# The z columns of a hybrid trunk's input projection, computed once for all heads by Strassen ahead of the heads

## The chip, the core and the metric

The kernel runs on one core of one Trainium2 chip. The metric is the time of one execution on the device in microseconds (us), the median of repeated runs. A NeuronCore has five engines with one instruction queue each: PE (TensorE, the matmuls), DVE (VectorE), ACT (ScalarE), POOL (GpSimd) and SP (SyncE, which only issues DMA transfers here). They meet only at semaphores.

## The reference, cut to what matters

One decoder layer over 1040 tokens (16 meta tokens and 1024 others) of width 1024. RMSNorm gives u; one projection gives everything the three branches read; z is 1024 columns of it and only gates the SSM branch.

```python
u = rmsnorm(h, norm_w[layer])
proj = jnp.einsum('bld,de->ble', u, w_in[layer])
(q, k, v, g_attn, c_b, c_c, c_h, g_conv, z, xbc, dt) = jnp.split(proj, IN_SPLIT_POINTS, axis=-1)
...
y_ssm = ssd_branch(z, xbc, dt, ...)      # ends in gated_group_rmsnorm(y, z, w): y * silu(z), then RMSNorm by group
...
h = h + jnp.einsum('ble,ed->bld', y, w_out[layer])
return rmsnorm(h, final_norm_w)[:, N_META:]
```

## The kernel before, in words

All data are float32. A product is made of three matmuls of rounded halves, high times high, high times low and low times high: ACT writes the high half (a cast to float32r), DVE or POOL the low half (source minus high). u is kept in SBUF for the whole kernel as `u_hi` and `u_lo`, 8 tiles of 128 columns of the model by 1040 tokens.

The program has three parts. Every engine walks the same written list of steps (`AHEAD`, then `BODY` for three heads, then `LAST`) and does those that are its own, in that order; nothing is reordered at run time, and semaphores alone hold an engine back.

1. The token stage (`ahead()`): for each of 9 token tiles `x_square` (ACT), `x_mean` (DVE), `x_power` (POOL), `x_scale` (DVE), `x_turn` (PE, eight transposes into PSUM), `x_high` (ACT) and `x_low` (DVE). Two tiles have PSUM room of their own (`u_ps`). Between the turns of the last tiles PE projects the first head's K and Q; `BEHIND` holds the other pieces of Q, K, V and the small dt products.
2. Four heads. In each, attention, and then a scan over 9 chunks (steps `chunk`, `decay`, `scan`, `carry`, `norm`, `ssm_out`). Between their steps `filler` deals out half pieces of projection (`project`: 12 matmuls of 342 to 512 columns), so that PE has work while the others answer. The head's 256 z columns are 8 steps `z` on PE, one for each 128 tokens, 24 matmuls of 256 columns each: three between the last attention steps, one ahead of `chunk` 0, and four as filler of the first chunks. ACT takes the tanh of each, DVE gates it into `z_n`. `PAUSE` puts empty units behind them.
3. The output projection, 2048 by 1024, by Strassen's method in seven products (`M_11` ... `M_22`, 8 slots each; `multiply` makes 3 matmuls of 512 columns for each of 4 token tiles).

DMA transfers are issued by SP in the order of the list: `load` for the weights of a projected tile (512 KB), `decay_load` for the scan, `x_load` and so on.

## Time and profile before

| | |
|---|---|
| time, median of 3 runs | 1036.84 us (1036.62 to 1036.87) |
| span of the profiled execution | 1035.9 us |
| PE busy | 1010.1 us (98%) |
| DVE, ACT, POOL busy | 622.6, 443.3, 253.3 us |
| matmuls | 6177 |

The span runs from the first to the last instruction of one profiled execution; the page gives no other time of that execution, and the median of the runs without a profile is 0.9 us longer. A busy share says how full an engine is, not who is waited for; for that there are the waits and the chain that ended last, a walk back from the last instruction to whatever released each step.

### The profile page before, as it was taken

What the parts mean: (1) busy time and instruction counts of PE and PEld (TensorE: products, weight loads), DVE (VectorE), ACT (ScalarE), POOL (GpSimd) and SP (SyncE); (2) the same over time, 40 slices, a digit from 0 to 9 for tenths busy, and PEclk for the clock granted to TensorE, in tenths of its full rate; (3) what the DMA queues carried; (4) which work ended last, traced back from release to release, by engine and by line L of the source; (5) the groups of instructions that cost most, each with busy time, mean ns of one, the idle gap of its engine ahead of it and who ended that gap; (6) DMA issues with size and microseconds to landing.
All of it is one profiled execution on the core that took longest, in us unless ns stands there. A gap on an engine that the chain in (4) does not pass through costs nothing.

```text
span 1035.9 us, 16326 instructions
## 1 busy us (share of the span) xinstructions
PE 1010.1 (98%) x6177; PEld 923.2 (89%) x6177; DVE 622.6 (60%) x1199; ACT 443.3 (43%) x1020; POOL 253.3 (24%) x222
## 2 busy tenths in 40 slices
PE   3999999999999999999999999999999999999997
PEld 3889989998999999989999999899999898888885
DVE  7555766446257664462576644625766536798866
ACT  6333444343434343434343344343433544543555
POOL 3012331233223412332224133322241330000002
PEclk8999999999999999999999999999999999999999
DMA  8012322221143232211422322114223203994313
GB/s 271 1 45 82 102 80 78 69 62 52 45 129 102 66 88 72 62 43 40 144 91 69 92 76 62 42 41 143 74 75 98 77 24 106 364 385 143 101 52 163
DMA packets 105945, 101.22 MB, mean 98 GB/s; under 512 B 6022, under 2 KB 79852, under 8 KB 105868
## 3 DMA queue, kind: packets, MB, share of 16 engines
q1 hardware_dynamic: 105868, 100.18, 30.2%
q8 instruction: 50, 0.82, 0.3%
q14 instruction: 27, 0.22, 0.1%
HBM read 79.11 MB, written 21.05 MB: 97 GB/s over the span
## 4 chain that ended last, share of the span: by engine, by line
PE 95%; DVE 2%; ACT 1%; issue 1%; DMA 1%; POOL 0%; DVEq 0%; SPq 0%; ACTq 0%
PE ps L1614 51%; PE ps L1623 15%; PE ps L1815 9%; PE ps L1599 5%; PE ps L1780 3%; PE ps L1829 2%; PE ps L1758 2%; PE ps L1759 2%; PE ps L1831 1%; PE ps L1835 1%; PE ps L1706 1%; PE ps L1781 1%; PE ps L1800 1%; DMA conv_u<-in_norm_w 1%; PE ps L1762 0%
## 5 line engine op out<-in xcount | busy, mean ns | idle before, releaser
L1614 PE MATMUL ps<-u_hi,w_hi 128*128 128x348 f32 (+3 forms) x1024 | 364.3, 356 | 1.8 <-POOL w_lo L908 1.8
L1614 PE MATMUL ps<-u_lo,w_hi 128*128 128x348 f32 (+3 forms) x1024 | 348.1, 340 | 0.0
L1614 PE MATMUL ps<-u_hi,w_lo 128*128 128x348 f32 (+3 forms) x1024 | 347.4, 339 | 0.0
L908 POOL TENSOR_TENSOR w_lo<-w_raw,w_hi 128x1024 fp32r<-128x1024 f32 (+1 forms) x56 | 122.8, 2193 | 343.7 <-ACT w_hi L998 271.7
L1614 PEld LDWEIGHTS ps<-u_hi,w_hi 128*128 128x128 f32 x1024 | 193.9, 189 | 13.5 <-POOL w_lo L908 2.1
L1614 PEld LDWEIGHTS ps<-u_hi,w_lo 128*128 128x128 f32 x1024 | 193.2, 189 | 11.0
L1614 PEld LDWEIGHTS ps<-u_lo,w_hi 128*128 128x128 f32 x1024 | 193.6, 189 | 10.3
L899 POOL TENSOR_TENSOR small<-small,m_half 128x1 f32<-128x1 f32 (+2 forms) x57 | 41.3, 727 | 332.0 <-DVE small L1553 143.0
L1388 DVE TENSOR_REDUCE small<-ps 128x1 f32<-128x144 f32 (+7 forms) x64 | 49.6, 774 | 90.4 <-PE ps L1762 89.9
L1815 PE MATMUL ps<-w_hi,u_hi 128*128 128x256 f32 x256 | 73.1, 286 | 0.0
L1815 PE MATMUL ps<-w_lo,u_hi 128*128 128x256 f32 x256 | 72.0, 281 | 0.0
L1815 PE MATMUL ps<-w_hi,u_lo 128*128 128x256 f32 x256 | 71.9, 281 | 0.0
L1090 ACT ACTIVATE work<-ps,small 128x144 f32<-128x144 f32 (+7 forms) x64 | 48.1, 751 | 53.8 <-DVE small L1388 53.8
L1122 ACT ACTIVATE y_n<-y_n,small 128x256 f32<-128x256 f32 x32 | 16.3, 509 | 116.5 <-POOL small L899 116.5
L1599 PE MATMUL ps<-ident,work 128*128 128x128 f32 (+2 forms) x369 | 55.7, 285 | 7.0 <-DVE work L1224 7.0
L1623 PE MATMUL ps<-q_hl 128*128 128x512 f32 x264 | 62.1, 389 | 0.0
L1623 PEld LDWEIGHTS ps<-q_hl 128*128 128x128 f32 x264 | 49.6, 188 | 10.3
L1599 PEld LDWEIGHTS ps<-ident,work 128*128 128x128 f32 (+2 forms) x369 | 43.7, 141 | 10.6 <-DVE work L1224 8.5
L1464 DVE TENSOR_TENSOR lm_buf<-lm_buf,cbm 128x512 f32<-128x512 f32 x32 | 22.1, 691 | 50.4 <-PE ps L1835 40.4
L998 ACT CAST w_hi<-w_raw 128x1024 fp32r<-128x1024 f32 x48 | 50.0, 1041 | 0.0
L1815 PEld LDWEIGHTS ps<-w_hi,u_hi 128*128 128x128 f32 x256 | 48.1, 188 | 1.3 <-issue 1.3
L1108 ACT ACTIVATE lm_buf<-acum_b,sg 128x128 f32<-128x128 f32 x128 | 40.8, 390 | 18.2 <-DMA acum_b<-acum_scratch 14.4
(302 smaller groups left out, 1741.1 us busy)
## 6 DMA issues: line engine op xcount, KB each, us to landing
w_raw<-in_w_in SPq DMA_DIRECT2D x56, 512.0 KB, 4.1
...
```

What stands on the lines that cost most here:

```text
L899: return eng.tensor_tensor(to[0:rows_, n:n + w], of[0:rows_, n:n + w], m_half[0:rows_, 0:w], ALU.pow)
L908: eng.tensor_tensor(w_lo[:, a % 2, ks, :], w_raw[:, a % 2, ks, :], w_hi[:, a % 2, ks, :].bitcast(F32), ALU.subtract).then_inc(w_lo_ok, 1)
L998: eng.copy(w_hi[:, b, :, :], w_raw[:, b, :, :]).then_inc(w_hi_ok, 1)
L1090: eng.activation(prob[m][:, 0:nk], s_ps[:, 0:nk], ACT.Exp, bias=mx[:, m:m + 1], accum_out=psum_e[:, s % 2, m:m + 1]).then_inc(exp_ok, 1)
L1108: ins = eng.activation(lmat[:, a % 2, r, :], acum_b[:, a % 2, r, :], ACT.Relu, bias=sg[:, 1, a, r:r + 1], scale=-1.0)
L1388: eng.tensor_reduce(mx[:, m:m + 1], s_ps[:, 0:nk], AX.X, ALU.max, negate=True).then_inc(max_ok, 1)
L1464: eng.tensor_tensor(lmat[:, b, :, :], lmat[:, b, :, :], cbm[:, b, :].unsqueeze(1).to_broadcast([P, R, P]), ALU.mult).then_inc(g_ok, 1)
L1599: return eng.transpose(dst, src, ident[0:n, 0:n])
L1614: ins = eng.matmul(dst, w[:, k, 0:m], u[:, k, cols], start=(k == 0 and n == 0), stop=(k == KD - 1 and n == 2))
L1623: ins = eng.matmul(ps[:, BANKS[n // KS][t], :], y[:, at], w, start=(begins and m == 0), stop=(ends and m == 2), skip_group_check=True)
L1780: eng.matmul(o_ps[:, P:2 * P], a_t[:, n, :], v_blk[:, n, :], start=(n == 0), stop=False)
L1815: ins = eng.matmul(pb[p % 2][:, 0:GW], u[:, k, ca:cb], w[:, :, k, :], start=(k == 0 and n == 0), stop=(k == KD - 1 and n == 2))
```

## The change

z no longer belongs to the heads. Between the token stage and the first head the whole of z, 1024 tokens by 1024 columns over a depth of 1024, is computed in Strassen's seven products of 512 by 512 by 512: `M_11`, `M_12`, `M_S2`, `M_S1`, `M_S3`, `M_S4`, `M_22`, each of 4 slots (a slot is one 128 deep step for 4 token tiles: 12 matmuls of 512 columns, `z_multiply`). The first two, 8 slots, are the steps `z_early` and need only u; the other five, slots 8 to 27, are in `z_run` and need sums of quarters of u (`s1`, `s2`, `s3`, each split into high and low) and of quarters of the weights (`z_sum`). Results are gated (`z_tanh`, `z_gate`) and stored to DRAM (`z_store`); each head reads its 1 MB back by one `z_load`. The heads' `z` steps are gone, the pieces of `TCB` stand in their places around the end of attention, and `PAUSE` is 1. In the token stage each tile now goes in two halves through one PSUM bank each, no projection stands between the turns, the splitting of z's weights stands among its steps, and Q, K, V of the first head come behind z (`PRE`). The lists `Z_ACT` and `Z_DVE`, not shown, write out the order of ACT and DVE in `z_run`.

```diff
+ZK = KD // 2
+Z_SLOTS = 7 * ZK
+ZX_BANKS, ZY_BANKS = (0, 1, 4, 7), (5, 6, 2, 3)
+Z_BANKS = (ZX_BANKS, ZY_BANKS, ZX_BANKS, ZX_BANKS, ZY_BANKS, ZX_BANKS, ZY_BANKS)
+Z_BLOCKS = {"T3": (0, 0), "T4": (1, 0), "T1": (0, 1), "T2": (1, 1)}
+Z_OF = ("T3", "T4", "T2", "T1", "T3", "T2", "T4")
+Z_TURNED = 8
+Z_OUT = ((0, 0), (1, 1), (0, 1), (1, 0))
+Z_READ = (M_12, M_S2, M_S3, M_S4, M_22)
+Z_EARLY = [(p, t, j) for p in (M_11, M_12) for t in range(4) for j in range(ZK)]
+Z_PER_TURN = 1
...
+def ahead():
...
+    early = list(Z_EARLY)
+    for r in range(-3, CH):
+        if 0 <= r:
+            out += [("x_high", (r, 0)), ("x_high", (r, 1))]
+        if r + 1 in range(CH):
+            out.append(("x_scale", r + 1))
+        if r + 2 in range(CH):
+            out += [("x_mean", r + 2), ("x_power", r + 2)]
+        out += [(name, arg) for name, arg, at in BETWEEN if at == r]
+        if r + 3 in range(CH):
+            out.append(("x_square", r + 3))
+        if 0 <= r:
+            out += [("x_low", (r, 0)), ("x_low", (r, 1))]
+        if r >= 5:
+            out.append(("s1", r - 5))
+        if r + 1 in range(CH):
+            out.append(("x_turn", (r + 1, 0)))
+            out += [("z_early", early.pop(0)) for _ in range(0)]
+            out.append(("x_turn", (r + 1, 1)))
+            out += [("z_early", early.pop(0)) for _ in range(Z_PER_TURN - 1 if r > 0 else 0)]
+    out += [("z_early", e) for e in early]
+    return [(name, arg, 1) for name, arg in out]
+
+
+BETWEEN = [("z_high", 0, 0), ("z_high", 1, 0), ("z_low", 0, 0), ("z_low", 1, 0), ("z_high", 2, 1), ("z_high", 3, 1), ("z_low", 2, 1), ("z_low", 3, 1),
+           ("z_high", 4, 2), ("z_low", 4, 2), ("z_high", 5, 3), ("z_low", 5, 3), ("z_high", 6, 4), ("z_low", 6, 4), ("z_high", 7, 5), ("z_low", 7, 5),
...
         if s == QB:
-            add("split", TZ1)
-            add("load", TCB)
-            add("load", TCC)
+            add("z_load")
...
-    add("z", 1)
...
-    units = [[("z", a, 0)] for a in range(5, QB + 1)]
-    units[-1].append(("split", TCB, 0))
-    units += [[]] * PAUSE
...
+    add("o_mean", 1)
+    emit(conv[0])
+    spare(1)
+    add("o_scale", 1)
+    emit(conv[1])
+    spare(2)
+    emit(conv[2])
+    add("attn_out", 1)
+    add("store_attn")
+    spare(9)
+    add("decay_load", 1)
+    add("decay_load", 2)
+    emit(conv[3])
+    add("chunk", 0)
+    add("decay", 1)
+    units = [[]] * PAUSE + conv[4:]
+    jobs = [(n + PAUSE - 4, job) for n, job in jobs]
+    if not last:
+        units += half_pieces([TQ, TK, TV], 1)[0]
...
-PAUSE = 4
+PAUSE = 1
...
+            def z_run():
+                iteration(-1, [("s2", 0, 1), ("s2", 1, 1), ("z_sum", ("T2", 1), 1), ("z_sum", ("T3", 0), 1), ("z_sum", ("T3", 1), 1),
+                               *[("s3", (M_S3, k), 1) for k in range(ZK)], ("z_sum", ("T4", 0), 1), ("z_sum", ("T4", 1), 1),
+                               *[("s3", (M_S4, k), 1) for k in range(ZK)]])
...
+                    elif step == "z_low":
+                        high, low = z_ring(a)
+                        eng.wait_ge(z_hi_ok, a + 1)
+                        eng.tensor_tensor(low, z_src(a), high.bitcast(F32), ALU.subtract).then_inc(z_lo1_ok, 1)
+                    elif step == "z_sum":
+                        name, half = a
+                        x, y, done = {"T1": ("T1", "T3", 0), "T2": ("T2", "T1", 1 + half), "T3": ("T2", "T3", 3 + half), "T4": ("T4", "T2", 3 + half)}[name]
+                        if name in ("T1", "T2"):
+                            eng.wait_ge(z_in[name], 32)
+                        if done:
+                            eng.wait_ge(z_sum_ok, done)
+                    elif step == "s3":
+
+                        p, k = a
+                        cols = slice(META + HALF, L) if p == M_S3 else slice(META, META + HALF)
+                        q = (M_S3, M_S4).index(p) * ZK + k
+                        if q == 0:
+                            eng.wait_ge(z_out_ok, 4)
+                            eng.wait_ge(s2d_ok, 2)
+                        if q >= 2:
+                            eng.wait_ge(s_lo_ok[M_S3 if q - 2 < ZK else M_S4], (q - 2) % ZK + 1)
+                        own(eng, eng.tensor_tensor(s_f[q % 2], u_hi[:, ZK + k, cols].bitcast(F32), s2_f[:, k, :], ALU.subtract))
+                        eng.tensor_tensor(s_f[q % 2], s_f[q % 2], u_lo[:, ZK + k, cols].bitcast(F32), ALU.add).then_inc(s3_ok, 1)
...
+                    elif step == "z_acc":
+
+                        o, t = a
...
+                        eng.copy(z_tmp[o][t], ps[:, ZX_BANKS[t], :]).then_inc(z_acc_ok, 1)
...
-                        eng.wait_ge(x_tr, a + 1)
-                        eng.copy(u_hi[:, :, ca:cb], u_ps[a % 2].rearrange("p (k n) -> p k n", k=KD)[:, :, 0:cb - ca]).then_inc(u_hi_ok, 1)
+                        eng.wait_ge(x_tr, 2 * a + h + 1)
+                        if a >= 5 and h == 0:
+                            eng.copy(s1_f[a - 5], u_ps[0])
+                        eng.copy(u_hi[:, ZK * h:ZK * (h + 1), ca:cb], u_ps[h].rearrange("p (k n) -> p k n", k=ZK)[:, :, 0:cb - ca]).then_inc(u_hi_ok, 1)
...
+                    elif step == "s1":
+
+                        eng.wait_ge(u_hi_ok, 2 * (a + 5) + 2)
+                        eng.tensor_tensor(s1_f[a], u_ps[1], s1_f[a], ALU.add).then_inc(s1_ok, 1)
...
-                            eng.wait_ge(bank_free[p % 2], it * (PPI // 2) + p // 2 + 2)
+                            eng.wait_ge(z_n_in, 16 * (it + 2))
...
+            def z_multiply(n, t):
+                p, j = divmod(n, ZK)
+                hi_u, lo_u = z_u(p, j, t)
+                hi_w, lo_w = z_ring(n)
+                terms = [(hi_u, hi_w), (hi_u, lo_w), (lo_u, hi_w)]
+                for m, (u, w) in enumerate(terms):
+                    ins = eng.matmul(ps[:, Z_BANKS[p][t], :], u, w, start=(p in BEGINS and j == 0 and m == 0),
+                                     stop=(j == ZK - 1 and m == 2), skip_group_check=True)
+                return ins
+            def z_run():
+                for n in range(Z_TURNED, Z_SLOTS):
+                    p, j = divmod(n, ZK)
+                    eng.wait_ge(z_lo_ok, n - Z_TURNED + 1)
+                    if p in (M_S3, M_S4):
+                        eng.wait_ge(s_lo_ok[p], j + 1)
+                    if p == M_S1 and j == 0:
+                        eng.wait_ge(s_lo_ok[p], 4)
...
+                        ins = z_multiply(n, t)
+                        if j == ZK - 1 and p in Z_READ:
+                            ins.then_inc(z_bank, 1)
+                    if not (j == ZK - 1 and p in Z_READ):
+                        ins.then_inc(z_k, 1)
...
-                        if a >= 2:
-                            eng.wait_ge(u_lo_ok, a - 1)
-                        for k in range(KD):
-                            ins = turn(u_ps[a % 2][:, k * P:k * P + n], x_buf[a][0:n, k * P:(k + 1) * P], n)
+                        if a >= 1:
+                            eng.wait_ge(u_lo_ok, 2 * a + h - 1)
+                        if a >= 6:
+                            eng.wait_ge(s1_ok, a - 5)
+                        for k in range(ZK):
+                            ins = turn(u_ps[h][:, k * P:k * P + n], x_buf[a][0:n, (ZK * h + k) * P:(ZK * h + k + 1) * P], n)
...
```

Three places of the order that the rows are read at. PE in the token stage, before; `work` and `lm_buf` hold the token tiles, x8 is eight transposes in a row:

```order
L1614 MATMUL ps<-u_hi,w_hi 128x348
L1614 MATMUL ps<-u_lo,w_hi 128x348
L1614 MATMUL ps<-u_hi,w_lo 128x348
L1599 MATMUL ps<-ident,lm_buf 128x128 x8
L1614 MATMUL ps<-u_hi,w_hi 128x348
L1614 MATMUL ps<-u_lo,w_hi 128x348
```

and after, from the program's start:

```order
L1870 MATMUL ps<-ident,ys 128x16 x8
L1870 MATMUL ps<-ident,work 128x128 x64
L1904 MATMUL ps<-w_hi,u_hi 128x512
L1904 MATMUL ps<-w_lo,u_hi 128x512
L1904 MATMUL ps<-w_hi,u_lo 128x512
L1904 MATMUL ps<-w_hi,u_hi 128x512
```

Before, 36 matmuls of the first head's K and Q stand between the turns of the last tiles; after, all 72 turns stand together and the first matmul of z comes behind the last of them.

POOL from the token stage's end to the first head, before (row L915 is part of the token stage):

```order
L915 TENSOR_TENSOR wd<-conv_g,wd 128x8x16
L899 TENSOR_TENSOR small<-small,m_half 128x1 x3
L908 TENSOR_TENSOR w_lo<-w_raw,w_hi 128x1024 x4
L944 TENSOR_TENSOR work<-work,acum_b 128x512
L908 TENSOR_TENSOR w_lo<-w_raw,w_hi 128x1024
```

and after, from the fifth sum of weights on; `lot` holds two sums of u at a time and `w_raw` the sum S2; a row of 1024 elements is half of a weight quarter:

```order
L1072 TENSOR_TENSOR th_tile<-th_tile,conv_b_s 128x1024
L1072 TENSOR_TENSOR conv_u<-conv_y,conv_u 128x1024
L1072 TENSOR_TENSOR acum_b<-th_tile,acum_b 128x1024
L1089 TENSOR_TENSOR lot<-u_hi,w_raw 128x512
L1090 TENSOR_TENSOR lot<-lot,u_lo 128x512
L1089 TENSOR_TENSOR lot<-u_hi,w_raw 128x512
L1090 TENSOR_TENSOR lot<-lot,u_lo 128x512
L1089 TENSOR_TENSOR lot<-u_hi,w_raw 128x512
```

In this stretch DVE has, after:

```order
L1487 TENSOR_TENSOR s_ys<-xdt,s_work 128x4x128
L1487 TENSOR_TENSOR s_ys<-xdd,s_work 128x4x128
L1487 TENSOR_TENSOR s_ys<-xd,s_work 128x4x128
L1487 TENSOR_TENSOR s_ys<-y_n,s_work 128x4x128
L1497 TENSOR_TENSOR w_lo<-conv_g,w_hi 128x512
L1493 TENSOR_TENSOR s_work<-lot,s_work 128x512
L1497 TENSOR_TENSOR w_lo<-conv_g,w_hi 128x512
L1493 TENSOR_TENSOR s_work<-lot,s_work 128x512
L1497 TENSOR_TENSOR w_lo<-conv_b_s,w_hi 128x512 x2
L1493 TENSOR_TENSOR s_work<-lot,s_work 128x512
L1497 TENSOR_TENSOR w_lo<-conv_u,w_hi 128x512
```

Every row here and in POOL's list reads two operands, both in SBUF. Before, POOL had nothing between the token stage and the weights of V; after, it has sixteen 512-element rows (`s3`) and two of 1024 (`T4`) that stand behind DVE's gate of the first result.

PE at the start of the last head's scan, before; `xdd` is what POOL makes of chunk 0:

```order
L1815 MATMUL ps<-w_hi,u_lo 128x256
L1599 MATMUL ps<-ident,work 16x128 x3
L1599 MATMUL ps<-ident,work 128x128 x3
L1800 MATMUL ps<-work 128x128
L1815 MATMUL ps<-w_hi,u_hi 128x256
L1815 MATMUL ps<-w_lo,u_hi 128x256
...
L1815 MATMUL ps<-w_hi,u_lo 128x256
L1835 MATMUL ps<-xdd,b_n 128x256
L1815 MATMUL ps<-w_hi,u_hi 128x256
```

and after:

```order
L1885 MATMUL ps<-u_hi,w_lo 128x512
L1870 MATMUL ps<-ident,work 16x128 x3
L1870 MATMUL ps<-ident,work 128x128 x3
L2116 MATMUL ps<-work 128x128
L2136 MATMUL ps<-xdd,lot 128x256
L1885 MATMUL ps<-u_hi,w_hi 128x342
L1885 MATMUL ps<-u_lo,w_hi 128x342
```

Before, a z step of 24 matmuls stood between the transposes of chunk 1 and the first product of the scan; after, nothing does. It is so in all four heads.

## Rows read from the trace of the kernel before

**Rows 1.** The page, its head and the line of busy times.
```profile
span 1035.9 us, 16326 instructions
...
PE 1010.1 (98%) x6177; PEld 923.2 (89%) x6177; DVE 622.6 (60%) x1199; ACT 443.3 (43%) x1020; POOL 253.3 (24%) x222
```

**Rows 2.** The waits of PE, whole execution.
```profile
PE ps L1599 <- DVE work L1224: 7.0, 4, 2.6
PE ps L1614 <- POOL w_lo L908: 1.8, 1, 1.8
```

**Rows 3.** The chain that ended last, in order of time: start, length, what.
```profile
25.64 3.29 PE ps L1614 x12
29.80 1.91 PE ps L1614 x12
...
36.23 2.79 PE ps L1614 x12
...
170.23 2.84 PE ps L1815 x24
```

**Rows 4.** The same chain, asked for from 885 us on.
```profile
884.96 143.99 PE ps L1623 x635
```

**Rows 5.** Timeline of PE, token stage: start, length, what.
```profile
23.67 1.97 PE L1599 MATMUL ps<-ident,work 128*128 128x128 f32 x8 [1.91 <-DVE work L1224]
...
35.20 1.04 PE L1599 MATMUL ps<-ident,ys 128*128 128x128 f32 x8
```

**Rows 6.** Timeline of ACT, token stage.
```profile
15.49 1.01 ACT L1011 CAST u_hi<-ps 128x1024 fp32r<-128x1024 f32 x1
16.39 1.06 ACT L1004 ACTIVATE conv_y<-work 128x1024 f32<-128x1024 f32 x1
...
17.45 1.03 ACT L998 CAST w_hi<-w_raw 128x1024 fp32r<-128x1024 f32 x1
```

**Rows 7.** Stretches: busy time by engine, clock, DMA share, GB/s.
```profile
0.00:12.00 12.00, 2.42 (x15) 2.34 (x16) 5.94 (x13) 6.08 (x10) 3.95 (x19) 1.00 0.82 273
12.00:18.00 6.00, 3.62 (x19) 2.59 (x17) 4.56 (x7) 5.41 (x8) 2.34 (x3) 1.00 1.08 348
```

**Rows 8.** Groups by shape: count, busy us, mean ns of one.
```profile
L1201 DVE TENSOR_TENSOR q_hl<-ys,q_hl 128x512 fp32r<-128x512 f32 x10 | 6.9, 694 | 1.7 <-ACT q_hl L976 1.7
```

**Rows 9.** Timeline of POOL, attention of the first head.
```profile
127.30 2.38 POOL L908 TENSOR_TENSOR w_lo<-w_raw,w_hi 128x1024 fp32r<-128x1024 f32 x1 [1.53 <-ACT w_hi L998]
129.65 2.31 POOL L944 TENSOR_TENSOR work<-work,acum_b 128x512 f32<-128x512 f32 x1
132.03 2.29 POOL L944 TENSOR_TENSOR work<-work 128x512 f32<-128x512 f32 x1
...
148.76 1.28 POOL L944 TENSOR_TENSOR acum_b<-acum_b,work 128x512 f32<-128x512 f32 x1
```

**Rows 10.** Timeline of DVE, same stretch.
```profile
125.99 1.30 DVE L1367 SCALAR_TENSOR_TENSOR work<-lm_buf,par_cw,work 128x1040 f32<-128x1040 f32 x1
...
128.34 2.44 DVE L1367 SCALAR_TENSOR_TENSOR work<-lm_buf,par_cw,work 128x1040 f32<-128x1040 f32 x1
...
131.94 1.24 DVE L1376 SCALAR_TENSOR_TENSOR work<-th_tile,work 128x1040 f32<-128x1040 f32 x1 [0.56 <-ACT th_tile L1076]
```

**Rows 11.** Timeline of DVE, token stage.
```profile
20.85 1.37 DVE L1298 TENSOR_TENSOR w_lo<-w_raw,w_hi 128x512 fp32r<-128x512 f32 x1
```

**Rows 12.** Timeline of PE, start of the first head's scan.
```profile
173.56 0.39 PE L1800 MATMUL ps<-work 128*128 128x128 f32 x2
...
176.72 0.69 PE L1835 MATMUL ps<-xdd,b_n 16*128 16x256 f32 x2
```

**Rows 13.** Timeline of DVE, same stretch.
```profile
173.52 0.42 DVE L1473 SCALAR_TENSOR_TENSOR work<-th_piece,ps 128x256 f32<-128x256 f32 x1 [0.77 <-ACT th_piece L1115]
173.86 0.41 DVE L1453 TENSOR_TENSOR xdt<-ps,sg 16x256 f32<-16x256 f32 x1
```

**Rows 14.** Timeline of POOL, same stretch.
```profile
174.34 1.18 POOL L923 TENSOR_TENSOR xdd<-xdt,sg 16x256 f32<-16x256 f32 x2 [10.07 <-DVE xdt L1453]
```

More of the change, by code:

```diff
@@ L155, with z_done, z_kept @@
 assert len(FIRST) == first_piece(TXS0)
-def ahead():
-    out = [("x_load", 0, 1), ("x_load", 1, 1), ("norm_load", 0, 1), ("x_load", 2, 1), ("x_load", 3, 1), ("load", 0, 1),
-           ("x_load", 4, 1), ("load", 1, 1), ("w_dt_load", 0, 1)]
-    out += [("x_load", a, 1) for a in range(5, CH)] + [("params_load", 0, 1)]
-    for r in range(-3, CH):
-        for name, lead in PIPE:
-            if 0 <= r + lead < CH:
-                out.append((name, r + lead, 1))
-        out += [(name, arg, 1) for name, arg, at in BETWEEN if at == r]
-    return out + [(name, arg, 1) for name, arg in BEHIND]
+ZK = KD // 2
[9 more added lines that the diff above has]
+Z_PER_TURN = 1
+def z_done(n):
+    p, j = divmod(n, ZK)
+    if p == M_11:
+        return "z_k", 1
+    if p in Z_READ and (j == ZK - 1 or p == M_12):
+        return "z_bank", 4 * (Z_READ.index(p) + 1)
+    return "z_k", 1 + sum(1 for m in range(2 * ZK, n + 1) if not (m % ZK == ZK - 1 and m // ZK in Z_READ))
+def z_kept(o, t):
+    return 4 * (0, 3, 1).index(o) + t + 1
 def piece(t, tc):
@@ L172, in piece @@
     return [("project", (p, 0)), ("project", (p, 1)), ("piece", p)]
-PIPE = (("x_high", 0), ("x_square", 3), ("x_scale", 1), ("x_mean", 2), ("x_low", 0), ("x_power", 2), ("x_turn", 1))
-BETWEEN = [("split", 0, 1), ("split_low", 0, 2), ("split", 1, 2), ("split_low", 1, 3), ("load", 2, 3), ("w_dt", 0, 3),
-           ("project", (first_piece(TK), 0), 4), ("project", (first_piece(TK), 1), 5),
-           ("project", (first_piece(TQ), 0), 6), ("project", (first_piece(TQ), 1), 7), ("dt_piece", 0, 7)]
@@ L411, in build @@
         k_hl = sb("k_hl", [P, 2, LP], F32R)
+        with nc.sbuf_tensor("s_work", [P, 4, 4 * HALF], F32R) as s_work:
+            pass
         work = sb("work", [P, 8324])
@@ L480, in build @@
         v_meta = sb("v_meta", [P, P])
+        with nc.sbuf_tensor("s_ys", [P, 4 * HALF], F32R) as s_ys:
+            pass
         ys = sb("ys", [P, 2, T])
```

397 lines of the change are left out of this document (279 added, 118 removed).

## The prediction

> **What bounds the kernel now.** I read the page first: PE is busy for 98% of the span and the others for 60% at most [rows 1], so matmul time counts unless a wait takes its place. PE's waits say where it is not full: it waits 7.0 us for the scaled token tiles and once 1.8 us for the low weights of V [rows 2]; the heads hold next to none. So two things decide: how much PE work goes, and whether PE can be kept as full in a stage that did not exist.
>
> The chain that ended last gives PE's pace, which durations do not, since matmuls overlap. A z step of 24 matmuls takes 2.84 us, 0.1185 us for 256 columns. A half piece of 12 takes 1.91 us at about 348 columns and 2.79 at 512 [rows 3]. In the output projection, which has the shape that z gets, 635 matmuls take 143.99 us, 0.2268 each [rows 4].
>
> **PE's work.** Removed: 32 z steps, 32 x 2.84 = 90.9 us. Added: 7 products x 4 slots x 12 = 336 matmuls of 512 columns, at the output projection's pace 76.2 us; at the half pieces' pace (2.79 / 12) it would be 78.1. I take the first, since the loop is the same. By the Trainium skill ("TensorE: Matmul & The Clock Gate", section "Wait — 56ns, not 53.3ns?") a warm matmul of 512 columns comes every 215.7 ns, which would make 72.5 us; no row here shows that pace. Strassen and wider matmuls thus save 14.7 us.
>
> **What the token stage hid.** Before, PE did 36 matmuls of K and Q between the last turns. The last turn starts at 35.20 [rows 5] and hands over 0.8 later, at 36.0; from there to the end are 999.9 us. After, the same 36 matmuls stand behind z and cost 1.91 + 1.91 + 2.79 = 6.6 us, which nothing hides. Before, the first 12 of them took 3.29 us instead of 1.91 [rows 3], as PE came out of the sparse stage at half its clock (1.2 GHz); z's first matmuls meet the same, and since this is now behind the 36.0 mark it costs a further 1.6.
>
> **When the turns end after.** A walk in order of each list. ACT casts a 1024-element tile in 0.90, and squares one in 1.06, start to start [rows 6]; two halves cost about 1.05, one 512-element cast 0.5. DVE's operations on 512 elements take 0.69, 0.6 start to start [rows 8]. ACT's first `z_high` needs block T3, the seventh transfer, 3.2 MB in; 273 GB/s over 12 us moved 3.3 MB [rows 7], so it starts at 12.3, and `x_square` 3 and tile 1's casts stand behind it: two `z_high` and the square end at 14.4. Tile 1 (casts, two `z_high`, square) takes 3.1, to 17.5. Tile 2 waits for T4, the twelfth transfer, 5.8 MB, at 19.3 by the 348 GB/s of the next stretch [rows 7], and ends at 20.9. Tiles 3 and 4 take 2.7 each: 26.3. From tile 5 on another loop is longer, because PSUM has one bank for each half and `s1` reads it too. Tile 5's copy, casts, `x_low` and `s1` end at 29.4. For tiles 6 and 7 the loop is four turns at their slow pace 1.0 (half of the 1.97 in [rows 5]), copy and cast 1.05, second cast 0.55, `x_low` 0.65, `s1` 0.65, signals 0.15: 4.05 each, 37.5. Eight turns of tile 8 end at 39.4.
>
> To that comes what POOL does to DVE. Both were asked for operations with two SBUF operands at once in [rows 9] and [rows 10]: DVE's tap, 1.30 when alone, takes 2.44 and ends 1.1 after POOL's 2.38; POOL's sum, 1.28 when alone, then takes 2.31 and ends 1.2 after DVE's; the next again waits for DVE's 1.24. They take turns. In the token stage too DVE's 0.69 became 1.37 beside POOL [rows 11]. The Trainium skill ("SBUF — State Buffer", section "🔬 SBUF: two separate sides") has such a rule: the port pair that the two share is locked for a whole instruction and the other blocks. By that rule, the trace agrees. Here `z_sum` of T1's second half (2.4 us) and `x_scale` 8 become ready together behind `x_power` 8. If DVE loses, the turns of tile 8 end at 41.6. I take 40.6, the middle, since no row says who wins such a start.
>
> **Inside z's seven products.** From E, the end of the turns: the slow start 1.6, then `M_11` and `M_12` of 48 x 0.2268 = 10.9 each; slots 8 to 11 (2.72 each) end at E + 34.3, slot 20 is due 8 x 2.72 later, at E + 56.1. `M_12`'s first tile is done at E + 15.2; behind it DVE has 20 operations until `z_gate` (0, 3), 12.6 us, E + 27.8. Only then may POOL begin `s3`, since the sums share `lot` with the tanh. Up to `z_low` 20, which slot 20 needs, POOL has 20 units of 512 elements and DVE 20 low halves, all with two SBUF operands, each side often needing the other's last. Taking turns, a pair costs 1.28 + 0.69 less the 0.16 by which two turns overlapped (131.96 to 134.32 is 2.36, against 1.28 + 1.24) = 1.81; 20 x 1.81 = 36.2, so `z_low` 20 ends at E + 64.0 and PE has waited 8 us by then. Were there no turns to take, POOL's 20 x 1.28 + 0.6 would end at E + 54.0, in time: zero. I take 7, as DVE is not always there to take its turn. Behind slot 20 all is done early. ACT has 60 operations of about 0.5 in the stage, which it hides; the DMA stores, the second read of T2 (issued about E + 45) and the heads' `z_load` (1 MB, some 20 us ahead of its use) hide too; the first head's weights are split during `M_22`, 11 us of PE work against 7.
>
> **In the heads.** `scan` 0 now follows the turns of chunk 1 at once. It needs `xdd`, made by POOL from DVE's `xdt`. Before, the PE went on to a z step after the turns at about 173.7 and the scan began at 176.72 [rows 12]. DVE's `xdt` stood behind a z gate and began at 173.86 [rows 13]; POOL's first `xdd` began at 174.34 and lasted half of 1.18 [rows 14]. Without the gate it ends at 174.5: PE waits 0.8 us, in four heads 3.2. If it does not wait in this way, zero; if the loss of cover costs the whole chain anew, 1.5 each. The last head's filler falls from 28 units to 16 over nine chunks; scan c - 1, the masked product, mean, power and scaling take about 2.2 us ahead of `ssm_out`, against one half piece of 1.9 between. Some 0.3 in six chunks, less 1.1 us that PE was idle there before: 0.7.
>
> **Sum.** 40.6 + 999.9 - 90.9 + 6.6 + 1.6 + 76.2 + 7.0 + 3.2 + 0.7 = 1044.9 us of span, against 1035.9 before; with the 0.9 by which the median stands above the span, 1045.8.
>
> **Rivals.** A change under 0.2% (2.1 us) cannot be told from none here.
> *The two engines do not collide in z.* For it: [rows 9] has DVE work with larger operations, and a DVE idle at the right time costs nothing. Against it: both lists are full there. Turns end at 39.4 and z waits 0.2: 1037.7, at the edge of no change.
> *The token stage is shorter.* My 39.4 is a sum of loops that I lengthened step by step; should ACT not wait for T3 and T4 and tiles 5 to 7 go at ACT's 2.7, the turns end at 33.5, and with no collision the time is 1031.8: faster. It decides from turns that end by 36.5 without collision, and by 29 with it, which I think impossible.
> *The filler is missed.* Each of the 32 chunk steps loses 0.25 us with fewer units between: 8 us more, 1053.8. Against it: before, chunks with empty units went by with hardly a wait.
> *No Strassen gain:* if wide matmuls with a changing stationary came at the half pieces' pace and each token tile's change of bank cost 0.08 (112 times 0.08 = 9 us), the time would be near 1056; [rows 4] has such changes and speaks against it.
>
> **How the numbers follow.** Forecast (collision, 1041 to 1050): 0.52. No collision: 0.16. Short token stage: 0.17. Filler missed or dear matmuls: 0.15. Range 1036.5 to 1053: it leaves out most of the faster case and half of the slowest. Faster takes the short token stage and a hundredth of the others, 0.18; same takes most of the second case, 0.12; slower 0.70.
>
> **What would show it.** Right: no matmul between the turns, the last turn ending near 40; slots 16 to 20 waiting for DVE's low halves, DVE's 0.69 and POOL's 1.28 stretched to about twice; four waits of 0.8 at the scan's first product; z's 336 matmuls near 76 us. Wrong: a token stage that ends by 36, or POOL and DVE at their lone durations in z.

## The result, and the profile of the changed kernel

The changed kernel takes 1056.14 us (median of 4 runs, 1055.10 to 1057.76) against 1036.86 for the kernel before (1036.62 to 1037.24): a ratio of 1.0186 (in brackets, here and below, the 95% interval: [1.0171, 1.0200]). It is slower, as forecast, but by 19.3 us where 8.9 were forecast, and outside the range of 1036.5 to 1053. The profiled execution took 1055.1, its span is 1053.3.

Of the 10.3 us between 1045.8 and 1056.14, 8.4 are in the span (1053.3 against 1044.9), and the rest of this document is about them. The other 1.9 is the conversion: in every run of either kernel the time is 1.7 to 1.8 us above the span of that run, and this profiled execution was the fastest of its four, so that the median stands 2.8 above its span. The 0.9 of the prediction came from a profiled execution that was itself 0.8 slower than the median.

The page, its head and its busy times, against [rows 1]:

```profile
span 1053.3 us, 15633 instructions
PE 1005.1 (95%) x5745; PEld 898.4 (85%) x5745; DVE 686.1 (65%) x1238; ACT 464.8 (44%) x1057; POOL 314.5 (30%) x250
```

PE is busy for 5.0 us less than before (1010.1) and the span is 17.4 longer: it is idle for 48.2 us instead of 25.8. The waits of PE, whole execution, against [rows 2]:

```profile
PE ps L1870 <- DVE u_lo L1468: 8.9, 5, 3.1
PE ps L1870 <- ACT y_n L1359: 7.2, 6, 3.8
PE ps L1904 <- DVE w_lo L1497: 4.4, 4, 2.1
PE ps L2136 <- POOL xdd L1104: 2.7, 4, 0.7
PE ps L1885 <- POOL w_lo L1059: 1.8, 1, 1.8
```

L1870 is a transpose: of token tiles where it waits for `u_lo`, of the normalised y (`ssm_out`) where it waits for `y_n`. L1904 is a z multiply, L2136 the scan's product with `xdd`. The second row was forecast at a fraction of its size. Of the kernel before, beside [rows 2], the same view has in its last head:

```profile
PE ps L1829 <- DVE lm_buf L1464: 0.7, 1, 0.7
PE ps L1599 <- ACT y_n L1122: 0.4, 2, 0.2
```

The timeline of PE says where the longest waits for `y_n` fall in the changed kernel:

```profile
858.91 0.44 PE L1870 MATMUL ps<-ident,y_n 128*128 128x128 f32 x2 [1.32 <-ACT y_n L1359]
867.36 0.69 PE L1870 MATMUL ps<-ident,y_n 128*128 128x128 f32 x2 [3.81 <-ACT y_n L1359]
...
886.19 0.44 PE L1870 MATMUL ps<-ident,y_n 128*128 128x128 f32 x2 [1.44 <-ACT y_n L1359]
```

All six are in the last head, the three not shown with 0.2 us each. To see how much each part of the program gained or lost, I use two marks that both timelines have: the 1.80 us wait of the first matmul of V, and the scan's first product in the first and in the last head. In the kernel before the product of the first head is at 176.72 [rows 12]; the first mark and the product of the last head:

```profile
63.00 0.43 PE L1614 MATMUL ps<-u_hi,w_hi 128*128 128x348 f32 x1 [1.80 <-POOL w_lo L908]
...
801.12 0.69 PE L1835 MATMUL ps<-xdd,b_n 16*128 16x256 f32 x2
```

Of the changed kernel:

```profile
159.08 0.43 PE L1885 MATMUL ps<-u_hi,w_hi 128*128 128x348 f32 x1 [1.80 <-POOL w_lo L1059]
...
270.60 0.67 PE L2136 MATMUL ps<-xdd,lot 16*128 16x256 f32 x2 [0.68 <-POOL xdd L1104]
...
829.20 0.67 PE L2136 MATMUL ps<-xdd,lot 16*128 16x256 f32 x2 [0.68 <-POOL xdd L1104]
```

- Up to the first mark: 159.08 - 63.00 = +96.1. Forecast, with the terms that stand ahead of it: 40.6 - 36.0 + 6.6 + 1.6 + 76.2 + 7.0 = +96.0.
- Three periods of a head: 558.60 against 624.40, so 65.8 less, or 21.9 a head. Forecast: 8 z steps of 2.84 less 0.8 of waiting, 21.9.
- The rest, which is one head's worth (from the mark to the first product, and from the last product to the end): 111.5 + 224.1 against 113.7 + 234.8, 12.9 less. Forecast: 22.7 - 0.8 - 0.7 = 21.2 less.

The whole miss of 8.3 us (8.4 by the unrounded spans) lies in the last line. The chain of waits, in order of time, around the longest wait:

```profile
854.20 2.70 POOL w_lo L1059
856.90 0.02 SPq L946
...
857.02 0.33 SPq L847
...
857.40 0.43 SPq L861
...
857.88 5.20 DMA acum_b<-acum_scratch
...
863.11 1.29 ACT lm_buf L1349 x4
...
866.22 0.56 POOL small L1047
...
866.80 0.52 ACT y_n L1359
...
867.36 0.69 PE ps L1870 x2
868.05 3.42 PE ps L1885 x12
```

Read it backwards. PE waits for `y_n`. Its norm stands in ACT's queue behind the exponentials of the next chunk's decay table, and these wait for the table's DMA, `decay_load` 6. That DMA was issued at 857.88, right behind the first load for the output projection (L847 and L861, `out_load` 0). And `out_load` 0 held SyncE's queue: it waits for the last `w_lo` split (tile GC), which POOL ends at 856.90. The order of the steps explains why this is new. In the kernel before, `out_load` 0 stood between `decay_load` 7 and 8; without z steps the convolution's half pieces stand earlier (four of them are ahead of `chunk` 0 now, where none was), the `out_load` steps are tied to these pieces, and `out_load` 0 now stands between `decay_load` 5 and 6, with three decay loads behind it instead of one. PE's clock adds to it. The stretches from 864 on:

```profile
864.00:866.00 2.00, 0.00 (x0) 0.00 (x0) 0.71 (x2) 1.92 (x7) 0.00 (x0) 0.92 1.08 354
866.00:868.00 2.00, 0.64 (x3) 0.64 (x4) 1.90 (x6) 1.20 (x4) 1.12 (x2) 0.50 0.95 313
868.00:870.00 2.00, 2.00 (x9) 2.00 (x8) 0.62 (x2) 1.97 (x7) 0.00 (x0) 0.50 0.04 11
870.00:872.00 2.00, 2.00 (x10) 1.94 (x9) 0.00 (x0) 0.05 (x1) 0.00 (x0) 0.50 0.00 0
872.00:874.00 2.00, 2.00 (x16) 1.92 (x15) 1.25 (x4) 0.00 (x0) 0.61 (x1) 0.87 0.00 0
```

(Stretch, length, busy time of PE, PEld, DVE, ACT, POOL with counts, granted clock, DMA share, GB/s.) The granted clock fell to 0.50, that is 1.2 GHz, within the wait of 3.8 us, near 865.7, and in stretches of half a microsecond it reads 0.50 up to 872.5 and 0.98 behind it, 5.1 us after PE's restart. The 12 matmuls that take 1.89 elsewhere in this head take 3.42. From the restart to the next transposes of y are 9.06 us, in the run late_loads below, without the half clock, 6.72: it costs about 2.3 us. (The expectation of late_loads has the half clock end at 873.6; 872.5 is what these stretches say.)

### The profile page after: what moved, and what is told of

The parts are those of the page before. It is cut to its first block, busy times and chain, and to the rows that moved or that the text cites. A ratio compares the mean times of both kernels' runs of the same rounds, so it can differ in the third digit from the quotient of the medians.

```text
span 1053.3 us, 15633 instructions
## 1 busy us (share of the span) xinstructions
PE 1005.1 (95%) x5745; PEld 898.4 (85%) x5745; DVE 686.1 (65%) x1238; ACT 464.8 (44%) x1057; POOL 314.5 (30%) x250
## 4 chain that ended last, share of the span: by engine, by line
PE 82%; issue 5%; POOL 5%; DVE 4%; ACT 2%; DMA 1%; SPq 0%; DVEq 0%; ACTq 0%; POOLq 0%
PE ps L1885 45%; PE ps L1894 14%; PE ps L1904 4%; PE ps L1870 4%; PE ps L2096 3%; PE ps L2130 2%; PE ps L2074 2%; PE ps L2075 2%; POOL w_lo L1059 1%; PE ps L2132 1%; PE ps L2136 1%; DVE work L1462 1%; DMA acum_b<-in_w_in 1%; POOL lot L1090 1%; POOL lot L1089 1%
## 5 line engine op out<-in xcount | busy, mean ns | idle before, releaser
L1059 POOL TENSOR_TENSOR w_lo<-w_raw,w_hi 128x1024 fp32r<-128x1024 f32 x48 | 117.5, 2449 | 293.4 <-ACT w_hi L1183 293.4
L1047 POOL TENSOR_TENSOR small<-small,m_half 128x1 f32<-128x1 f32 (+2 forms) x57 | 46.0, 809 | 311.7 <-DVE small L1824 143.9
L1870 PE MATMUL ps<-ident,work 128*128 128x128 f32 (+2 forms) x393 | 62.6, 297 | 16.4 <-DVE u_lo L1468 8.9
L1870 PEld LDWEIGHTS ps<-ident,work 128*128 128x128 f32 (+2 forms) x393 | 49.2, 148 | 22.4 <-issue 12.4
L1743 DVE TENSOR_TENSOR lm_buf<-lm_buf,lot 128x512 f32<-128x512 f32 x32 | 24.3, 761 | 58.6 <-PE ps L2136 41.9
L1894 PEld LDWEIGHTS ps<-q_hl 128*128 128x128 f32 x264 | 49.6, 188 | 10.3
L1104 POOL TENSOR_TENSOR xdd<-xdt,sg 128x256 f32<-128x256 f32 (+1 forms) x32 | 21.0, 660 | 63.7 <-DVE xdt L1732 63.7
L2096 PE MATMUL ps<-conv_b_s,conv_g 128*128 128x128 f32 x288 | 39.3, 282 | 0.0
L2074 PE MATMUL ps<-k_hl,q_hl 128*128 128x512 f32 (+4 forms) x112 | 37.8, 338 | 0.2
L2075 PE MATMUL ps<-k_hl,q_hl 128*128 128x512 f32 (+4 forms) x112 | 36.3, 335 | 0.0
```

The lines of the kernel that those rows point to most:

```text
L1047: return eng.tensor_tensor(to[0:rows_, n:n + w], of[0:rows_, n:n + w], m_half[0:rows_, 0:w], ALU.pow)
L1059: eng.tensor_tensor(w_lo[:, a % 2, :, :], w_raw[:, a % 2, :, :], w_hi[:, a % 2, :, :].bitcast(F32), ALU.subtract).then_inc(w_lo_ok, 1)
L1870: return eng.transpose(dst, src, ident[0:n, 0:n])
L1894: ins = eng.matmul(ps[:, BANKS[n // KS][t], :], y[:, at], w, start=(begins and m == 0), stop=(ends and m == 2), skip_group_check=True)
L2074: eng.matmul(s_ps[:, at:end], q_hi[m][:, qs], k_st[m][:, at:end], start=True, stop=False)
L2075: ins = eng.matmul(s_ps[:, at:end], q_lo[m][:, qs], k_st[m][:, at:end], start=False, stop=not masked)
```

## The experiments

Theory Q (queue): the loss in the last head is the order in SyncE's queue. Theory F (filler): it is the smaller number of half pieces between a chunk's scan and the transposes of its y.

**late_loads.** A single move in SyncE's order:

```diff
 LAST = schedule(True)
+LOADS = [step for step in LAST if step[0] == "out_load" and step[1] < EARLY]
+LAST = [step for step in LAST if step not in LOADS]
+LAST[LAST.index(("decay_load", CH - 1, 0)) + 1:LAST.index(("decay_load", CH - 1, 0)) + 1] = LOADS
```

> The changed kernel with one thing moved: in the last head the output projection's first four loads (two DMAs each) are issued by SyncE behind decay_load 8 and no longer between decay_load 5 and 8. TensorE's order, the half pieces and every other engine are as in the changed kernel. Theory Q (queue): in the changed kernel out_load 0 waits in SyncE's queue until w_lo of tile GC is written at 856.9, decay_load 6 is issued behind it at 857.9 and lands at 863.1, the normalised y of that chunk is late, TensorE stands 3.8 us at 867.4 and then runs at half clock to 873.6, which costs 2.4 more. With the loads behind, the 3.8 and the 2.4 go, and perhaps 1 of the other 3.4 us of waits for y_n: 1047 to 1050. Theory F (filler): the waits for y_n come because the last head has fewer half pieces between a chunk's scan and the transposes of its y: then they stay, 1055 to 1057.

Measured 1051.63 (1.0136 [1.0121, 1.0151] of before), 4.5 below the changed kernel, between the ranges of Q and F and nearer to Q's. The timeline of PE, all its waits for `y_n` of 0.3 us or more:

```profile
861.18 0.44 PE L1873 MATMUL ps<-ident,y_n 128*128 128x128 f32 x2 [1.32 <-ACT y_n L1362]
...
882.51 0.44 PE L1873 MATMUL ps<-ident,y_n 128*128 128x128 f32 x2 [1.44 <-ACT y_n L1362]
```

The wait of 3.8 is gone and so is the half clock; from the last head's first product to the end are 218.2 us instead of 224.1, 5.9 less. (The span gained only 3.6, because this execution came to the last head's first product 2.3 us later. Of that, 1.6 lie behind V's first matmul: after the same wait of 1.80 us the granted clock fell to 0.50 from about 160 to 163.5 here, and stayed at 1.00 in the profiled execution of the changed kernel. The other 0.6 stands ahead of the mark and has no cause that I know.) The 1.32 and the 1.44 stay. So Q holds for about two thirds of the miss in the span. Q's further 1 us from the other waits did not come.

**turns5.** `Z_PER_TURN = 5` in place of 1: four z multiplies behind each pair of turns.

> The changed kernel with four z multiplies (three matmuls each, 0.70 us) behind each pair of turns of tiles 2 to 8 of the token stage, 28 steps in place of none; nothing else moves. Theory: TensorE is idle for 2.3 to 2.5 us of each turn round of 4.5 us there, so that most of the 28 x 0.70 = 19.5 us are hidden; the turns come later by about 0.3 us a round, and waits for the low part of u or of the weights may cost another 2: gain 13 to 17, 1039 to 1043. Rival: the turns' rounds are as long as TensorE's new work and its waits together, because each z multiply waits for the low part of u of the tile before, which is itself what ends the round: the stage grows by 2 us or more in each of the seven rounds, gain 5 or less, 1051 or more.

Measured 1051.29 (1.0132 [1.0117, 1.0147]): 4.9 less, at the rival's price but not in its way. The turns' rounds grew by some 0.3 us each, as the theory had it (the last turns start at 41.33 instead of 39.49), not by 2; what was lost is PE's idle time behind them:

```profile
45.13 1.19 PE L1904 MATMUL ps<-q_hl,u_hi 128*128 128x512 f32 x2 [2.74 <-DVE y_n L1473]
57.26 0.80 PE L1904 MATMUL ps<-w_hi,k_hl 128*128 128x512 f32 x1 [4.10 <-DVE w_lo L1497]
73.30 0.47 PE L1904 MATMUL ps<-w_hi,s_work 128*128 128x512 f32 x1 [3.31 <-DVE w_lo L1497]
```

With 28 of the 32 early steps gone, 4 steps are all that covers the 14.9 us from the end of the turns (42.4) to the first matmul with the S2 block (57.26), and the granted clock is 0.66 in 40 to 50 and 0.84 in 50 to 60.

**pool_half.** One of the two GpSimd operations of each `s3` step left out, so that the low part of u is missing in these sums (indices shortened).

```diff
-own(eng, eng.tensor_tensor(s_f[q % 2], u_hi[...].bitcast(F32), s2_f[:, k, :], ALU.subtract))
-eng.tensor_tensor(s_f[q % 2], s_f[q % 2], u_lo[...].bitcast(F32), ALU.add).then_inc(s3_ok, 1)
+eng.tensor_tensor(s_f[q % 2], u_hi[...].bitcast(F32), s2_f[:, k, :], ALU.subtract).then_inc(s3_ok, 1)
```

> The changed kernel with GpSimd's second operation of each of the eight s3 steps left out (the low part of u isn't added, 8 operations of 1.6 us between 69 and 103): part of the z computation is missing. Theory of the shared turns: DVE's operations with two SBUF operands take 1.78 us in place of 0.69 while GpSimd is at work, each waiting for one GpSimd operation, and so z_low comes late and TensorE waits 4.4 us for w_lo in this stage. With half of the GpSimd operations gone these waits fall to 1 or less: 1051.5 to 1053. Rival: DVE is late by its own count of operations or by ScalarE's casts, and the waits stay: 1055 to 1057.

Measured 1049.63 (1.0122 [1.0104, 1.0139]), 6.5 less and 1.9 below the forecast range; no wait for the low halves of z's weights is left, and the mark of V's first matmul comes at 153.43, 5.65 earlier. The rival is out.

**s3_dve.** The `s3` block moved from the GpSimd function to the VectorE one, and in the order lists:

```diff
-*[("s3", (M_S3, k), 1) for k in range(ZK)]      # and of M_S4, GpSimd's list
+Q3 = [(p, k) for p in (M_S3, M_S4) for k in range(ZK)]
+at = Z_DVE.index(("z_gate", (0, 3))) + 1
+Z_DVE[at:at] = [("s3", Q3[0]), ("s3", Q3[1])]
+for q in range(2 * ZK - 2):
+    Z_DVE.insert(Z_DVE.index(("s3_low", Q3[q])) + 1, ("s3", Q3[q + 2]))
```

> The changed kernel with the eight s3 steps (16 operations of two SBUF operands each) taken from GpSimd and put on VectorE, each two places ahead of its s3_low; the four sums of weights stay on GpSimd. Nothing is left out. Theory of the shared turns: what costs is not the number of operations but GpSimd's 1.1 us share in each of VectorE's; VectorE alone needs 25 x 0.69 + 16 x 0.69 = 28 us between 69 and 105, and so keeps up with TensorE's 36: the waits for w_lo fall from 4.4 to 0 to 2: 1049.5 to 1052. Rival: VectorE is the engine that is short there, by its count; 16 operations more make z_low later still and the waits grow: 1057 to 1062.

Measured 1048.66 (1.0108 [1.0093, 1.0123]), 7.5 less and 1 us better than expected. The same stretch of the changed kernel, then of this one:

```profile
70.00:105.00 35.00, 30.56 (x128) 23.36 (x127) 32.76 (x22) 15.00 (x28) 30.84 (x18) 1.00 0.17 47
```
```profile
70.00:105.00 35.00, 35.00 (x153) 28.58 (x152) 32.10 (x51) 20.72 (x38) 0.00 (x0) 1.00 0.35 103
```

DVE is busy for 32 us in both. With GpSimd at work that is 22 operations, without it 51. The timelines of DVE, changed kernel and s3_dve:

```profile
79.30 3.48 DVE L1497 TENSOR_TENSOR w_lo<-conv_b_s,w_hi 128x512 fp32r<-128x512 f32 x2
82.70 1.78 DVE L1493 TENSOR_TENSOR s_work<-lot,s_work 128x512 fp32r<-128x512 f32 x1
84.41 2.90 DVE L1497 TENSOR_TENSOR w_lo<-conv_u,w_hi 128x512 fp32r<-128x512 f32 x1
```
```profile
79.02 0.69 DVE L1494 TENSOR_TENSOR lot<-lot,u_lo 128x512 f32<-128x512 f32 x1
79.63 1.29 DVE L1503 TENSOR_TENSOR w_lo<-conv_b_s,w_hi 128x512 fp32r<-128x512 f32 x2
```

So it is not the number of operations. Each DVE operation carries about one GpSimd operation's time: 0.69 becomes 1.78 beside the sums of `s3` (512 elements, 1.28 when alone), 2.90 beside one of 1024.

**pause0.** `PAUSE = 0`: all half pieces of the scan stage one place earlier.

> The changed kernel with PAUSE 0 in place of 1: the first half piece of each head's scan stage stands between chunk 1 and scan 0 on TensorE, and each of the next ones one place earlier. By the term of the prediction, scan 0 waits 0.7 to 0.8 us in each of four heads for xdd, and a half piece of 1.9 us ahead of it covers that: 2.7 less, 1052.5 to 1054.5. Rival: the half piece is missing where it was taken away (each ssm_out waits for the normalised y by as much), and the time stays within 1 us of 1056, or grows in the last head.

Measured 1063.75 (1.0260 [1.0243, 1.0278]), 7.6 more, which neither side had expected in size. The four waits for `xdd` are gone, as forecast, but in the last head:

```profile
871.50 0.44 PE L1870 MATMUL ps<-ident,y_n 128*128 128x128 f32 x2 [3.99 <-ACT y_n L1359]
...
891.02 0.69 PE L1870 MATMUL ps<-ident,y_n 128*128 128x128 f32 x2 [4.36 <-ACT y_n L1359]
```

The second of them is new, with a granted clock of 0.50 in 890 to 894 behind it. That is theory F's mechanism: in this head, cover moved by one half piece (2.8 us) makes a wait of 1.44 one of 4.36. It isn't the last head alone, though: `y_n` is waited for 11 times instead of 6, in all 13.5 us instead of 7.2, and 1.3 us of that stand in each of the other heads, which had none.

**before_noz.** The kernel before with the z steps' matmuls cut from 24 to 1, so that z is wrong. The step's wait for the low weights, which stood in the middle of the 24, now stands ahead of the one.

```diff
-for k in range(KD):
...
-    for n, (u, w) in enumerate(terms):
-        ins = eng.matmul(pb[p % 2][:, 0:GW], u[:, k, ca:cb], w[:, :, k, :], ...)
+ins = eng.matmul(pb[p % 2][:, 0:GW], u_hi[:, 0, ca:cb], w_hi[:, :, 0, :], start=True, stop=True)
```

> The kernel before with 23 of the 24 matmuls of each of the 32 z steps left out (z is wrong by this; the transposes, tanh and gate stay). It measures what the heads give when the z matmuls go and nothing is added or moved: by the profile's rows 32 x 2.84 = 90.9, less 32 x 0.13 for the matmul that stays: 86.7, so 950 if nothing waits. Theory Q: the order in SyncE's queue is the one of before, so little is lost in the last head: 950 to 954. Theory F, that the z matmuls covered chains of the scan: 957 or more, with new waits in every head.

Measured 1023.02 (0.986 [0.9846, 0.9875]): only 14.3 less, where 86.7 us of matmuls are gone. Q's range of 950 to 954 is out; F's "957 or more, with new waits in every head" holds, but says nothing of the 66 us that it is more. PE's waits:

```profile
PE ps L1813 <- DVE work L1473: 20.2, 12, 2.7
PE ps L1599 <- DVE work L1376: 15.7, 4, 3.9
...
PE ps L1599 <- DVE conv_y L1422: 7.0, 4, 1.8
PE ps L1813 <- POOL w_lo L908: 2.9, 4, 0.7
```

These rows make 45.8 us in four heads (the last, 2.9, is the wait that the edit moved), and some 20 us in each head are at half clock, in the first head:

```profile
165.00:175.00 10.00, 5.08 (x17) 3.46 (x17) 7.65 (x14) 2.41 (x6) 1.21 (x2) 0.50 0.36 107
175.00:185.00 10.00, 6.84 (x26) 6.04 (x27) 5.47 (x14) 5.95 (x17) 2.45 (x3) 0.52 0.18 54
```

Half of the 11.9 busy us of these two stretches is lost to the clock, which I estimate at 24 us in four heads; with the 45.8 that is near the 72 that are missing. The z matmuls were the cover of the gates, of the convolution's end and of the split. The change takes the cover away, but takes the gates out of the heads as well and puts `conv` half pieces in the cover's place; its first three heads gain the full 21.9 us each. (Whether that is due to the gates or to the half pieces, no run separates.)

**Combinations.** all3 is late_loads, s3_dve and pause0; all4 adds turns5. turns3 is `Z_PER_TURN = 3`. two is late_loads and s3_dve, three adds turns3, four shifts the last head's half pieces to one place later:

```diff
-    units = [[]] * PAUSE + conv[4:]
-    jobs = [(n + PAUSE - 4, job) for n, job in jobs]
+    units = [[]] * (PAUSE + last) + conv[4:]
+    jobs = [(n + PAUSE + last - 4, job) for n, job in jobs]
```

> late_loads, s3_dve and pause0 together. If the three act at different places, their gains add: 4.5 (measured for late_loads) + 5.5 (s3_dve as forecast) + 2.7: 1043.4, between 1041.5 and 1045.5. If the residual waits of the last head grow with PAUSE 0, 1045 to 1048.

> all3 with turns5 added (four z multiplies behind each pair of turns). turns5 alone gained 4.8 of the 19.5 us of matmuls that it moved, because its waits for what VectorE and GpSimd make (w_lo, s_work) grew by 4 and TensorE ran at half clock between 40 and 60. With s3 off GpSimd, GpSimd is free sooner and these waits should be a little shorter: 5 to 8 below all3, 1036 to 1040. If they are set by s2 and the token stage's last tiles, as much as in turns5: 4 to 5 below all3.

> The changed kernel with two z multiplies behind each pair of turns of tiles 2 to 8 (14 steps of 0.70 us), where turns5 had four (28 of the 32 early steps). Theory: in turns5 only 4 early steps stood behind the last turn, and TensorE then waited for the S2 block of u (made by VectorE and GpSimd within some 12 us of the last turn): 4.1, 3.3 and 2.7 us and half clock between 40 and 60. With 14 moved, 18 steps or 12.6 us stand there and cover it, and two multiplies fit into each turn round's idle 2.3 us: gain 7 to 9.8, 1046 to 1049. Rival: the turns wait longer in each round as soon as TensorE is given anything: gain 5 or less, 1051 or more.

> late_loads and s3_dve together, PAUSE as in the changed kernel. They act in the last head and in the z stage, so their measured gains add: 4.5 and 7.5: 1043 to 1045. all3, which has the same two and PAUSE 0, gave 1052.0; so PAUSE 0 alone costs 7 to 9 here too, as it did in pause0 (7.6), if it is the last head's half piece that was taken away and not the queue that costs there. If PAUSE 0 costs only together with the late decay loads, two is within 2 us of all3.

> two with turns3 added. If turns3's gain is independent of the others: two less 7 to 9.8, that is 1034 to 1037, about the time of the kernel before (1036.9). If s3 on VectorE makes it the bound when the z stage starts earlier: 1038 to 1042.

> three with the half pieces of the last head's scan stage one place later (PAUSE 2 there, 1 in the other heads). pause0 had them one place earlier and its waits for y_n in the last head grew from 7.2 to about 11.5 us. If the last head is short of half pieces at its end (chunks 5 to 8), one more there takes 1.4 of the 3.6 us of waits that late_loads left: 1 to 2 below three. If instead each place is as short as the next, the wait moves to where the piece was taken (chunk 1 or 2): within 1 us of three.

| kernel | median us | ratio to before |
|---|---|---|
| all3 | 1051.98 | 1.0146 [1.0131, 1.0161] |
| all4 | 1052.50 | 1.0146 [1.0128, 1.0163] |
| turns3 | 1048.36 | 1.0104 [1.0090, 1.0118] |
| two | 1044.20 | 1.0060 [1.0045, 1.0075] |
| three | 1042.41 | 1.0046 [1.0033, 1.0058] |
| four | 1042.28 | 1.0044 [1.0032, 1.0057] |

Three of the combinations missed their forecasts: all3 was to take 1041.5 to 1048; all4 was to be 4 to 8 below all3 and is 0.5 above it (PE waits 8.3 us for one low half in it); three is 0.4 above the worse of its two ranges.

two came as expected: the gains of late_loads and s3_dve add (1056.1 - 4.5 - 7.5 = 1044.1), and all3, which differs from it in PAUSE alone, is 7.8 above it. So PAUSE 0 costs the same with the late loads as without, and is F's doing, not Q's. In the profiled executions the two are 7.0 apart, and half of that, 3.6, lies in the three periods ahead of the last head: 187.4 us a head in all3, 186.2 in two. turns3 gained 7.8 alone, as forecast, but in three only 1.8 on top of two: PE then waits 4.2 us for `w_lo`, at 60.09, where neither two nor turns3 has a wait:

```profile
60.09 0.50 PE L1913 MATMUL ps<-w_hi,k_hl 128*128 128x512 f32 x1 [4.20 <-DVE w_lo L1506]
```

In three, POOL's two sums for T4 (2.85 us at 51.94 and 2.80 at 54.76) run there because the `s3` steps that stood ahead of them are gone, and beside them DVE's S2 subtractions, which stand ahead of that low half, take 2.89 and 2.73. The clock takes a part too: V's first matmul comes 2.8 us earlier in three than in two, but behind its wait of 1.80 us the granted clock fell to 0.50 in three and not in two, and 1.6 of the 2.8 are lost again. four waits 1.1 us less for `y_n` (2.5 against 3.6: the wait of 1.33 is 0.2) and 0.7 more for `lm_buf`, no change of the time that could be told.

**five and six.** five is three with POOL's T4 sums held back; six is five with POOL's split of tile GC behind a norm in the last head.

```diff
+if name == "T4":
+    eng.wait_ge(s_lo_ok[M_S4], 2)
```
```diff
+order = [step for step in LAST if step != ("split", TGC, 0)]
+order.insert(order.index(("norm", 3, 0)) + 1, ("split", TGC, 0))
+iteration(HEADS - 1, order)
```

> three with GpSimd's two sums for the weight block T4 held back until the second low block of s3 for M_S4 is made (near 90 us), where VectorE is ahead of TensorE. In three these two sums (2.85 and 2.80 us at 51.94 and 54.76) run beside VectorE's S2 subtractions, which take 2.89 and 2.73 in place of 0.69, and TensorE waits 4.2 us for w_lo at 60.09. If that is the place where turns3's gain went in three, the wait falls below 1 and the time by 3 to 5: 1037.5 to 1039.5. If the S2 chain is late because of the sums of T2 and T3, which stay, it falls by 1 or less: 1041.5 to 1043.

> five with GpSimd's split of the weights of tile GC in the last head put behind the power of the norm of chunk 3 in GpSimd's queue (it stood ahead of it and of xdd; it takes 2.4 to 2.7 us). If the wait of 1.3 us for y_n of that chunk is this queue's doing, it goes and the others stay: 1 to 1.3 below five. If it is short cover on TensorE (theory F), the wait stays and the time is that of five within 0.5.

five took 1043.87 (1.0063 [1.0050, 1.0077]), 1.5 more than three where 3 to 5 less were expected. Its place was right: the wait of 4.2 us is gone and the S2 subtractions are back at 0.69. But two waits have come up behind:

```profile
69.22 0.47 PE L1915 MATMUL ps<-w_hi,s_work 128*128 128x512 f32 x1 [2.03 <-ACT xdt L1222]
96.13 0.50 PE L1915 MATMUL ps<-w_hi,q_hl 128*128 128x512 f32 x1 [2.84 <-DVE w_lo L1508]
```
```profile
94.73 0.62 ACT L1194 CAST w_hi<-conv_y 128x512 fp32r<-128x512 f32 x1 [9.42 <-DMA th_tile<-in_w_in]
```

The row of 94.73 is ACT's: the second read of T2 may start only when all sums are made, so holding back T4 held back the DMA, and ACT's cast stood for 9.4 us until it had landed. What a sum blocks is not only the product that uses it. The first wait (2.03) is the one that three has with 0.46, moved up by the gain.

six took 1044.08 (1.0061 [1.0048, 1.0074]), the same as five. The wait of 1.33 us for `y_n` is gone, as the queue would have it, and the next one grew from 0.20 to 0.75. From V's first matmul to the end are 888.9 us where five has 888.4, which looks like no gain; but the last head, from its first product with `xdd` to the end, takes 217.2 us against 218.2. The 1.5 between is lost right behind V's first matmul, where the clock fell in six and not in five (stretches of six, then of five):

```profile
153.00:155.00 2.00, 2.00 (x9) 2.00 (x8) 0.00 (x0) 0.00 (x0) 1.66 (x1) 0.50 0.91 244
```
```profile
154.00:156.00 2.00, 2.00 (x16) 2.00 (x14) 0.00 (x0) 0.00 (x0) 2.00 (x1) 1.00 0.62 165
```

So in the profiled execution the last head gained the 1.0 that was expected, and the medians, which differ by 0.2, don't show it. four, which put one more half piece there, took the same wait away without touching POOL: either cure does.

The best versions, three and four, stand about 5 us above the kernel before (ratio 1.0045): none beat it.

## Why the prediction was right in sign and wrong in size

- **End of the turns (40.6).** z's first matmul starts at 41.09. Right, 0.5 late. POOL won the start against `x_scale` 8 (DVE's 1.27 took 2.87 from 34.69 on), the branch that I had at 41.6, so the loops ahead of it were 0.5 shorter than mine.
- **The 336 matmuls (76.2).** Mis-sized by 1.7. The chain of the last products:

```profile
103.30 22.27 PE ps L1904 x96
```

  That is 0.2320 each, so 77.9, the pace of the half pieces and not that of the output projection [rows 4]. The Trainium skill's 215.7 ns for a warm matmul of 512 columns ("TensorE: Matmul & The Clock Gate", section "Wait — 56ns, not 53.3ns?") isn't reached here either.
- **The slow start (1.6).** The first 96 took 23.06 instead of 22.27: 0.8.
- **Shared turns (7.0).** The mechanism and the stretching were right, the place only in part: PE waits at slots 18, 19 and 20 for 2.3 us, but the longest wait, 2.15 at 77.72, is at slot 12, behind the four `s1_low` of DVE, where I had none. The size is 4.4 in named waits and 5.6 by the mark that pool_half and s3_dve moved. The rule of the Trainium skill ("SBUF — State Buffer", section "🔬 SBUF: two separate sides"), by which one of the two blocks for a whole instruction of the other, is what s3_dve shows: 22 operations against 51 in the same busy time.
- These four errors cancel (+0.5, +1.7, -0.8, -1.4), and K and Q cost what was said, so that the sum up to the mark came out at 96.1 against 96.0. That it is so near is luck.
- **Heads (-90.9, +3.2).** 21.9 a head, and four waits of 0.7 for `xdd` where 0.8 was said. Right. What I had not seen, and before_noz shows, is that the matmuls cut alone would not have given this term: other work has to fill the place, or the gates have to go with them.
- **The last head's filler (0.7): the step that failed.** I wrote "some 0.3 in six chunks", counted PE's half pieces alone, and read only PE's list there. (The count was crooked as well: 28 units has the four empty ones in it, 16 leaves out the one; filled units are 24 and 16.) The waits for `y_n` come to 7.2, the half clock behind them to 2.3; less 0.7 us of a wait for `lm_buf` and 0.4 for `y_n` that PE had before, 8.4. Of this, 5.9 is SyncE's queue with its half clock (late_loads), in which `out_load` 0 was carried ahead of `decay_load` 6 and 7 by the half piece to which it is tied, so that three decay loads stood behind its wait. The other 2.5 are the waits that late_loads has left (3.6, less those 1.1 of before), the 1.32 and the 1.44 above all. The 1.32 goes when POOL's split stands behind the norm (six, 1.0 us in the last head) or when a half piece stands ahead of it (four). The 1.44 is short cover at least in this sense, that one half piece less ahead of it adds 2.9 (pause0, all3); no run puts one more there. 8.4 against the 0.7 of the term makes 7.7 of the 8.3 us; 0.6 stays unassigned. The time missed by 1.9 us more for the reason given in the section on the result.
- **Rivals.** "The filler is missed" named 1053.8, near the time, but as 0.25 us in each of 32 chunks; three heads lost nothing and the last lost it all. "Dear matmuls" named 1056 for a reason that explains 1.7 us. The two faster cases are out: the turns end at 41 and the collision is there.
